# Four low-part subtractions of the recurrent mixer's weights made by GpSimd instead of VectorE, counted by VectorE

## The chip, the core and the metric

The kernel runs on one core of one Trainium2 chip. The metric is the device time of one execution in microseconds (us), taken as the median of several executions.

## The reference, cut to what matters

The whole computation is a stack of blocks over a sequence of 256 rows of width 1024. The part that the change touches is the recurrent mixer of the first layer. With `x` the normalised rows (256 x 1024), it computes:

```python
def recurrent_mixer(x, w_in, conv_w, conv_b, gate_a_w, gate_a_b, gate_x_w, gate_x_b, lam, w_out):
    y, r = jnp.split(x @ w_in, 2, axis=-1)
    y = jax.nn.gelu(y)
    r = causal_depthwise_conv(r, conv_w, conv_b)
    h = rg_lru(r, gate_a_w, gate_a_b, gate_x_w, gate_x_b, lam)
    return (y * h) @ w_out
...
    # rg_lru
    gate_a = jax.nn.sigmoid(block_diag_linear(xf, w_a, b_a))
    gate_x = jax.nn.sigmoid(block_diag_linear(xf, w_x, b_x))
    log_a = -LRU_C * gate_a * jax.nn.softplus(-lam)
    a = jnp.exp(log_a)
    mult = jnp.sqrt(-jnp.expm1(2.0 * log_a))
    bx = xf * gate_x * mult
    # h[t] = a[t] * h[t-1] + bx[t], a scan over the sequence
```

Ahead of it stands a feed-forward part (`in01`, `out01`) and behind it another one (`in02`, `out02`), then the second layer and two layers of an attention and mLSTM block.

## The kernel before, in words

**Weights in units.** All weight matrices are streamed once, in 456 units numbered in the order of use. A unit is a block of up to 4 x 128 rows and 256 columns, held as 128 partitions x 1024 elements. A ring of four slots holds it three times: `raw` (as loaded), `w_hi` (rounded by ScalarE, line 951) and `w_lo` = `raw` - `w_hi` (a subtraction on VectorE, line 1478). TensorE multiplies each unit in three products (`w_hi` by `x_hi`, `w_hi` by `x_lo`, `w_lo` by `x_hi`, lines 541 to 543), which is 24 matmuls of 256 columns, 12 for each of two output tiles. Two units that share their columns make a pair.

**The counts of the ring.** `lo_made` counts `w_lo` units in their order. TensorE's unit U waits until `lo_made` is U+1, and SyncE issues the load of unit U+4 then, since the slot of `raw` is free. `hi_made` counts `w_hi` units for the engine that subtracts. `unit_done` counts units that TensorE has finished; ScalarE waits for it before it writes `w_hi` of unit U+4 over that of unit U.

**The order on each engine is written out by hand**, and each engine runs its own list in order. In the mixer, `x @ w_in` (`rec_b` and `rec_a`) has 16 units, steps r = 0 to 15 of a loop over pairs p = 0 to 7. They are units 68 to 83; `rec_out` (`@ w_out`) is units 84 to 91. At step r ScalarE and VectorE make the high and the low part of unit 68 + r + 3 (`LEAD` = 3), and after the second unit of a pair VectorE takes its two tiles out of PSUM (`scaled`, line 1518, `work<-bank,rstd`). VectorE also has the mixer's own work: `conv1(p)` (lines 1631 and 1633, at r = 1, 3, 5, 7), `mult_squares` (line 1644, at r = 9 and 12), `scans` (products of line 1652, scans of line 1655, at r = 12, 13, 14), `outputs` (line 1661) and `lower` (`y_lo`, line 1489), from r = 14 on. TensorE's gate products (lines 631 and 632) stand after steps 3, 5, 7 and 8 and wait for `conv1`.

**GpSimd in the mixer** has one list: four products (line 1368) when ScalarE's gates are there, four squares of `rec_a` (line 1373, `a2_new`) behind ScalarE's exponentials (line 1059), and the same again for channels 4 to 7. Then it waits for `rec_out`. `mult_squares` on VectorE waits for `a2_new`, ScalarE's square root (line 1066) for `mult_squares`, the scans for the square root, and `rec_out`'s products for `y_hi` and `y_lo` of the eight channels: unit 84 for channels 0 to 3, unit 85 for channels 4 to 7.

Of the kernel before, what the change touches and what calls it, by code (L numbers as in the profile page):

```python
# [16 lines left out]
RING = 4  # L17
# [78 lines left out]
def plan():  # L96

    units, pairs, phases = [], [], {}

    def phase(name, src, layer, rows, cols):  # L100
        ub, pb = len(units), len(pairs)
        for c0 in cols:
            ks = []
            k = 0
            while k < rows:
                n = min(KU, rows - k) if rows - k != 6 else 3
                ks.append((k, n))
                k += n
            pairs.append([(len(units) + j, k0, n) for j, (k0, n) in enumerate(ks)])
            units.extend((src, layer, k0, n, c0) for k0, n in ks)  # L110
        phases[name] = (ub, pb, len(cols))

    wide = range(0, D, CU)
    for l in range(DEPTH):
        for f in (1, 2):
            gate_up = [c + s * FF for c in range(0, FF, CU) for s in (0, 1)]
            phase(f"in{l}{f}", f"ffn{f}_w_in", l, NC8, gate_up)
            phase(f"out{l}{f}", f"ffn{f}_w_out", l, NF, wide)
            if f == 1:
                m = ("rec", "sg")[l]  # L120
                phase(m + "_b", m + "_w_in", 0, NC8, [D + c for c in wide])
                phase(m + "_a", m + "_w_in", 0, NC8, wide)
                phase(m + "_out", m + "_w_out", 0, NC8, wide)
    for l in range(DEPTH):
        for n, c in (("kv", [C_KV]), ("mif", [C_MIF]), ("aq", [C_AQ + c for c in wide]),
                     ("mqk", [C_MQK + c for c in wide]), ("mv", [C_MV + c for c in wide]),
                     ("mo", [C_MO + c for c in wide]), ("ag", [C_AG + c for c in wide]),
                     ("mg", [C_MG + c for c in wide])):
            phase(f"{n}{l}", "w_in_2", l, NC8, c)
        phase(f"proj{l}", "w_out_2", l, 2 * NC8, wide)  # L130
    return units, pairs, phases


UNITS, PAIRS, PHASES = plan()
# [34 lines left out]
GATES_AT = (3, 5, 7, 8)  # L169


def build_stack(nc: bass.Bass, consts, x, ffn1_norm, ffn1_w_in, ffn1_w_out, mix_norm, ffn2_norm, ffn2_w_in, ffn2_w_out,
                rec_w_in, rec_conv_w, rec_conv_b, rec_gate_a_w, rec_gate_a_b, rec_gate_x_w, rec_gate_x_b, rec_lambda,
                rec_w_out, sg_w_in, sg_v_norm, sg_w_s, sg_b_s, sg_w_out, final_norm, meta_2, norm_g_2, w_in_2,
# [2 lines left out]
    fp32, fp32r = mybir.dt.float32, mybir.dt.float32r  # L177
    ALU, ACT = mybir.AluOpType, mybir.ActivationFunctionType
    MUL, ADD, SUB, MAX, MIN = ALU.mult, ALU.add, ALU.subtract, ALU.max, ALU.min
# [5 lines left out]
    with ExitStack() as ctx:  # L185
        def sb(name, shape, dt=fp32):
            return ctx.enter_context(nc.sbuf_tensor(name, shape, dt))

        def sem(name):
            return ctx.enter_context(nc.semaphore(name))  # L190
# [4 lines left out]
        raw = sb("raw", [P, RING, KU, CU])  # L195
        w_hi = sb("w_hi", [P, RING, KU, CU], fp32r)
        w_lo = sb("w_lo", [P, RING, KU, CU], fp32r)
# [30 lines left out]
        def region(slots, width=L):  # L228
            o = at[0]
            at[0] += slots * width  # L230
            assert at[0] <= WORK_SLOTS * L, at[0]
            return work[:, o:o + slots * width].rearrange("p (c n) -> p c n", n=width)
# [9 lines left out]
        decay = region(12, NC8)  # L242
# [55 lines left out]
        w_loaded = [sem(f"w_loaded{i}") for i in range(RING)]  # L298
        hi_made = sem("hi_made")
        lo_made = sem("lo_made")  # L300
        unit_done = sem("unit_done")
        first_done = sem("first_done")
        tile_read = sem("tile_read")
# [82 lines left out]
        def _(sp):  # L386
# [50 lines left out]
            def straight(name, first=0):  # L437
                ub, pb, npairs = PHASES[name]
                for pr in range(pb + first, pb + npairs):
                    for U, _, n in PAIRS[pr]:  # L440
                        src, l, k0, n, c0 = UNITS[U]
                        a = dram[src][l]
                        if name == "out01":

                            for dst, s_ in small[2 * (U - ub):2 * (U - ub) + 2]:
                                sp.dma_start(dst, s_).then_inc(sg_loaded, 16)
                        if name.startswith("mif"):

                            sp.wait_ge(lo_made, U - RING + 1)
                            for g in range(2):  # L450
                                sp.dma_start(raw[:, U % RING, 0:n, 32 * g:32 * g + 4],
                                             a[k0 * P:(k0 + n) * P, c0 + 4 * g:c0 + 4 * g + 4].rearrange(
                                                 "(k p) n -> p k n", p=P)).then_inc(w_loaded[U % RING], 16)
                            continue
                        load(U, a[k0 * P:(k0 + n) * P, c0:c0 + CU].rearrange("(k p) n -> p k n", p=P),
                             U - RING + 1 if U >= RING else None)

            def gate_up(name):

                ub, pb, _ = PHASES[name]  # L460
                src, l, _, _, _ = UNITS[ub]
                cols = dram[src][l].rearrange("(s k p) (f j n) -> s f j p k n", k=KU, p=P, f=2, n=CU)
                first = 1 if ub == 0 else 0

                def turn(i):
                    for j in range(4):
                        U = ub + j
                        wait = U - RING + 1 + 4 * i
                        load(U, cols[j % 2, j // 2, i], None if isinstance(i, int) and wait <= 0 else wait)

                if first:
                    turn(0)
                    parameters()
                with sp.Fori(first, FF // CU) as i:
                    turn(i)
# [840 lines left out]
        def _(pool):  # L1316
            nc.gpsimd.memset(ones[:, :], 1.0)
            nc.gpsimd.memset(epsc[:, :], EPS).then_inc(ones_set, 1)
            TT = nc.gpsimd.tensor_tensor
# [7 lines left out]
            def squares(src, wait, T0, done, chunks=NC8 - 1):  # L1327

                for c in range(chunks):
                    wait(c)  # L1330
                    if c == 0:
                        link(TT(sumsq[:, T0:L], src(c), src(c), MUL))  # L1332
                    else:
                        link(TT(sq[:, T0:L], src(c), src(c), MUL))  # L1334
                        i_ = TT(sumsq[:, T0:L], sumsq[:, T0:L], sq[:, T0:L], ADD)
                        if c < chunks - 1:
                            link(i_)
                        else:
                            i_.then_inc(done, 1)

            def h_squares(n, name, T0):

                pb = PHASES[name][1]
                if n:
                    pool.wait_ge(sum_done, n + (n == 7))
                squares(lambda c: h[:, c, T0:L], lambda c: pool.wait_ge(tile_read, 2 * pb + c + 1), T0, sq_done)

            def gate_scale(f):

                def turn(i):  # L1350
                    for m in range(2):
                        pool.wait_ge(silu_done, 22 * f + m + 1 + 2 * i)
                        TT(ffn_r[:, m, :], ffn_s[:, m, :], rstd[:, META:L], MUL).then_inc(gate_scaled, 1)  # L1353
                with pool.Fori(0, FF // CU) as i:
                    turn(i)
# [6 lines left out]
            gate_scale(0)  # L1362
            h_squares(1, "out01", META)

            for b in (0, 4):
                for c in range(b, b + 4):
                    pool.wait_ge(gates_sig, 2 * c + 2)
                    TT(rec_x[:, c, :], rec_x[:, c, :], rec_g[:, c, :], MUL).then_inc(gated_in, 1)
                if b:
                    pool.wait_ge(mult2, 4)  # L1370
                for c in range(b, b + 4):
                    pool.wait_ge(ax_new, c + 1)
                    TT(rec_s[:, c % 4, :], rec_a[:, c, :], rec_a[:, c, :], MUL).then_inc(a2_new, 1)
            h_squares(2, "rec_out", META)
            gate_scale(1)
            h_squares(3, "out02", META)
# [84 lines left out]
        def _(dve):  # L1461
            V = nc.vector
            TT, TS, STT = V.tensor_tensor, V.tensor_scalar, V.scalar_tensor_tensor
# [8 lines left out]
            def split_w(U, off=0):  # L1472

                if U >= NU:
                    return
                n, s = UNITS[U][3], U % RING
                dve.wait_ge(hi_made, U + 1 + off)
                TT(w_lo[:, s, 0:n, :], raw[:, s, 0:n, :], w_hi[:, s, 0:n, :].bitcast(fp32), SUB).then_inc(lo_made, 1)  # L1478
# [188 lines left out]
            r = 0  # L1667
# [114 lines left out]
            for l in range(DEPTH):  # L1782
# [297 lines left out]
                for ph in STREAM:  # L2080
                    pb = PHASES[f"{ph}{l}"][1]
                    for p in range(PHASES[f"{ph}{l}"][2]):
                        pr = pb + p
                        for j, (U, _, _) in enumerate(units_of(pr)):
# [9 lines left out]
                            if len(steps) == 1 and steps[0][0] == "ml" and steps[0][1][1] == 0:  # L2094
                                kind, n = steps[0]
# [32 lines left out]
            for g in (2, 3):  # L2128
                c0, n, _ = OUT_GROUPS[g]
# [30 lines left out]
```

## Time and profile before

| | us |
|---|---|
| three runs | 1537.73, 1538.11, 1539.76 |
| their median | 1538.11 |
| profiled execution, device time | 1541.56 |
| profiled execution, span from the first to the last instruction | 1539.8 |
| mean granted TensorE clock in it, share of full speed | 0.988 |

The profiled execution took 1.8 us more than its span, which is what lies around the instructions, and 3.5 us more than the median of the three runs. Starts in the trace are us from the start of the span; the mixer's 16 steps and the first two units of `rec_out` lie between 208 and 281 us. In the rows PE is TensorE, PEld its weight loads, DVE VectorE, ACT ScalarE, POOL GpSimd and SPq SyncE's DMA queue. Most of the mixer's tiles are regions of one tensor and are called `work` there.

### The profile page before, as it was taken

To read this page: it belongs to the slowest core of one execution; us is meant where nothing else is said; L and a number is where in the kernel's file an instruction comes from. 1 tells how busy PE (TensorE), PEld (TensorE's weight loads), DVE (VectorE), ACT (ScalarE), POOL (GpSimd) and SP (SyncE) were. 2 spreads that over 40 slices of the span, in tenths; PEclk is the share of its full clock that TensorE was granted. 3 is DMA by queue.
4 is the path that set the end of the run, shared out by engine and by line. 5 is a ranking of instruction groups with operands and counts; after the bars stand their busy time and mean duration, and the time that the engine had idled before them with its cause. 6 is when DMAs were issued, how large, how long until landed. Compare 5 with 4: busy or idle time off the path is not lost.

```text
span 1539.8 us, 31458 instructions
## 1 busy us (share of the span) xinstructions
PE 1488.7 (97%) x11949; PEld 1467.5 (95%) x11949; DVE 1050.3 (68%) x2004; ACT 768.7 (50%) x1276; POOL 293.7 (19%) x361
## 2 busy tenths in 40 slices
PE   7999998999999999999999998999999999999998
PEld 7999998999999999999999997899999999899898
DVE  6666578766655666557766655888768768976883
ACT  5444458554545554454554534446744453566442
POOL 4111112211111111113311112343200125331000
PEclk9999999999999999999999999899999999999999
DMA  6656744555555655555565554443333554334333
GB/s 203 188 177 199 243 161 132 164 182 176 184 175 185 191 178 179 170 184 165 163 188 176 179 180 126 126 120 97 97 111 109 164 139 137 101 106 117 109 121 121
DMA packets 245276, 239.66 MB, mean 156 GB/s; under 512 B 15160, under 2 KB 244392, under 8 KB 245048
## 3 DMA queue, kind: packets, MB, share of 16 engines
q1 hardware_dynamic: 245176, 238.29, 50.8%
q8 instruction: 67, 1.10, 0.3%
q14 instruction: 33, 0.27, 0.1%
HBM read 237.21 MB, written 1.05 MB: 155 GB/s over the span
## 4 chain that ended last, share of the span: by engine, by line
PE 85%; DVE 10%; ACT 2%; issue 2%; POOL 1%; DMA 0%; SPq 0%; DVEq 0%; ACTq 0%; POOLq 0%
PE bank L541 25%; PE bank L543 25%; PE bank L542 25%; DVE w_lo L1478 3%; PE bank L865 1%; PE bank L805 1%; PE bank L823 1%; PE bank L788 1%; ACT w_hi L951 1%; DVE work L1518 1%; DVE work L1633 1%; PE bank L871 1%; PE bank L881 1%; PE bank L804 0%; DVE rstd L1496 0%
## 5 line engine op out<-in xcount | busy, mean ns | idle before, releaser
L1478 DVE TENSOR_TENSOR w_lo<-raw,w_hi 128x1024 fp32r<-128x1024 f32 (+1 forms) x456 | 557.7, 1232 | 317.8 <-ACT w_hi L951 317.4
L541 PE MATMUL bank<-x_hi,w_hi 128*128 128x256 f32 (+1 forms) x2480 | 721.8, 291 | 7.1 <-DVE x_lo L1491 5.2
L543 PE MATMUL bank<-x_hi,w_lo 128*128 128x256 f32 (+1 forms) x2480 | 708.8, 286 | 0.0
L542 PE MATMUL bank<-x_lo,w_hi 128*128 128x256 f32 (+1 forms) x2480 | 708.3, 286 | 0.0
L951 ACT CAST w_hi<-raw 128x1024 fp32r<-128x1024 f32 (+1 forms) x456 | 466.2, 1031 | 273.5 <-PE bank L543 256.8
L541 PEld LDWEIGHTS bank<-x_hi,w_hi 128*128 128x128 f32 x2480 | 477.9, 193 | 10.3 <-issue 6.8
L542 PEld LDWEIGHTS bank<-x_lo,w_hi 128*128 128x128 f32 x2480 | 478.2, 193 | 1.0
L543 PEld LDWEIGHTS bank<-x_hi,w_lo 128*128 128x128 f32 x2480 | 477.5, 193 | 0.0
L541 PE MATMUL bank<-y_hi,w_hi 128*128 128x256 f32 (+1 forms) x1088 | 310.4, 285 | 8.4 <-DVE y_lo L1489 8.3
L543 PE MATMUL bank<-y_hi,w_lo 128*128 128x256 f32 (+1 forms) x1088 | 309.8, 285 | 0.0
L542 PE MATMUL bank<-y_lo,w_hi 128*128 128x256 f32 (+1 forms) x1088 | 309.7, 285 | 0.0
L541 PEld LDWEIGHTS bank<-y_hi,w_hi 128*128 128x128 f32 x1088 | 209.3, 192 | 9.4 <-DVE w_lo L1478 4.4
L543 PEld LDWEIGHTS bank<-y_hi,w_lo 128*128 128x128 f32 x1088 | 209.4, 193 | 0.0
L542 PEld LDWEIGHTS bank<-y_lo,w_hi 128*128 128x128 f32 x1088 | 209.2, 192 | 0.0
L1353 POOL TENSOR_TENSOR work<-work,rstd 128x256 f32<-128x256 f32 x88 | 63.6, 742 | 415.1 <-ACT work L987 415.1
L1518 DVE TENSOR_TENSOR work<-bank,rstd 128x256 f32<-128x256 f32 (+1 forms) x204 | 81.7, 422 | 17.1 <-PE bank L543 16.7
L997 ACT CAST y_hi<-work 128x256 f32 (+1 forms) x88 | 35.6, 408 | 90.3 <-DVE work L1534 90.2
L987 ACT ACTIVATE work<-work 128x256 f32<-128x256 f32 x88 | 36.1, 419 | 78.3 <-DVE work L1518 78.3
L1334 POOL TENSOR_TENSOR sq<-h 128x256 f32<-128x256 f32 (+1 forms) x48 | 33.5, 698 | 199.2 <-DVE h L1563 196.9
L958 ACT ACTIVATE x_hi<-h,par 128x256 fp32r<-128x256 f32 (+1 forms) x64 | 32.8, 514 | 70.2 <-DVE h L1563 62.7
L1491 DVE SCALAR_TENSOR_TENSOR x_lo<-h,par,x_hi 128x256 fp32r<-128x256 f32 (+1 forms) x64 | 36.3, 569 | 29.9 <-ACT x_hi L958 29.8
L1332 POOL TENSOR_TENSOR sumsq<-h 128x256 f32<-128x256 f32 (+1 forms) x8 | 4.9, 618 | 248.1 <-DVE h L1563 240.8
(269 smaller groups left out, 1250.4 us busy)
## 6 DMA issues: line engine op xcount, KB each, us to landing
raw<-in_ffn_w_in_dram SPq DMA_DIRECT2D x176, 512.0 KB, 3.7
raw<-in_w_in_dram SPq DMA_DIRECT2D x100, 512.0 KB, 3.6
raw<-in_ffn_w_out_dram SPq DMA_DIRECT2D x64, 512.0 KB, 4.2
raw<-in_w_out_dram SPq DMA_DIRECT2D x32, 512.0 KB, 3.8
raw<-in_ffn_w_out_dram SPq DMA_DIRECT2D x32, 384.0 KB, 3.1
raw<-in_rec_w_in_dram SPq DMA_DIRECT2D x16, 512.0 KB, 3.6
raw<-in_sg_w_in_dram SPq DMA_DIRECT2D x16, 512.0 KB, 3.5
raw<-in_rec_w_out_dram SPq DMA_DIRECT2D x8, 512.0 KB, 3.4
```

Source lines behind the costliest of these rows:

```text
L541: mm(acc, wh, xh, start=first and j == 0, stop=False)
L542: mm(acc, wh, xl, start=False, stop=False)
L543: i_ = mm(acc, wl, xh, start=False, stop=last and j == n - 1)
L951: nc.scalar.copy(w_hi[:, s, 0:n, :], raw[:, s, 0:n, :]).then_inc(hi_made, 1)
L958: i_ = activation(xview(dst, k, N), src, ACT.Copy, scale=scale)
L987: activation(ffn_s[:, m, :], ffn_t[:, m, :], ACT.Silu).then_inc(silu_done, 1)
L997: nc.scalar.copy(dst, ffn_h[:, m, :]).then_inc(act_hi, 1)
L1334: link(TT(sq[:, T0:L], src(c), src(c), MUL))
L1353: TT(ffn_r[:, m, :], ffn_s[:, m, :], rstd[:, META:L], MUL).then_inc(gate_scaled, 1)
L1478: TT(w_lo[:, s, 0:n, :], raw[:, s, 0:n, :], w_hi[:, s, 0:n, :].bitcast(fp32), SUB).then_inc(lo_made, 1)
L1491: i_ = STT(out=xview(dst_lo, k, N), in0=src, scalar=scale, in1=hi, op0=MUL, op1=SUB)
L1518: TT(dst, tile(pr, m, N), rstd[:, T0:L], MUL).then_inc(tile_read, 1)
```

## The change

GpSimd makes `w_lo` of four units: 78, 82, 84 and 86 (`POOL_LO`). It makes 78 after its first four squares, and the other three one behind the other after its second four squares. Each waits for that unit's `hi_made` and raises a new semaphore, `pool_lo`. VectorE leaves these four out, at steps r = 7, 11, 13 and 15. At the next step, before it subtracts the following unit, it waits for `pool_lo` and raises `lo_made` by a one-column memset on an unused column, so that `lo_made` still counts units in order. No DMA is added or removed, and no operation moves on TensorE, ScalarE or SyncE.

```diff
+POOL_LO = [PAIRS[PHASES["rec_b"][1]][0][0] + r for r in (10, 14, 16, 18)]
...
         lo_made = sem("lo_made")
+        pool_lo = sem("pool_lo")
...
+            def split_w(U):
+
+                n, s = UNITS[U][3], U % RING
+                pool.wait_ge(hi_made, U + 1)
+                TT(w_lo[:, s, 0:n, :], raw[:, s, 0:n, :], w_hi[:, s, 0:n, :].bitcast(fp32), SUB).then_inc(pool_lo, 1)
+
             for b in (0, 4):
...
                 for c in range(b, b + 4):
                     pool.wait_ge(ax_new, c + 1)
                     TT(rec_s[:, c % 4, :], rec_a[:, c, :], rec_a[:, c, :], MUL).then_inc(a2_new, 1)
+                for U in POOL_LO[1:] if b else POOL_LO[:1]:
+                    split_w(U)
...
                 if U >= NU:
                     return
+                if isinstance(off, int) and U + off in POOL_LO:
+                    return
+                if isinstance(off, int) and U + off - 1 in POOL_LO:
+                    dve.wait_ge(pool_lo, POOL_LO.index(U + off - 1) + 1)
+                    V.memset(decay[:, 10, 0:1], 0.0).then_inc(lo_made, 1)
                 n, s = UNITS[U][3], U % RING
                 dve.wait_ge(hi_made, U + 1 + off)
```

On GpSimd, its whole list in the mixer reads before:

```order
L1368 TENSOR_TENSOR work<-work 128x256 [waits gates_sig] x4
L1373 TENSOR_TENSOR work<-work 128x256 [waits ax_new] x4
L1368 TENSOR_TENSOR work<-work 128x256 [waits gates_sig] x4
L1373 TENSOR_TENSOR work<-work 128x256 [waits ax_new,mult2]
L1373 TENSOR_TENSOR work<-work 128x256 [waits ax_new] x3
```

and in the changed kernel, whose line numbers are up to 17 higher:

```order
L1378 TENSOR_TENSOR work<-work 128x256 [waits gates_sig] x4
L1383 TENSOR_TENSOR work<-work 128x256 [waits ax_new] x4
L1373 TENSOR_TENSOR w_lo<-raw,w_hi 128x1024 [waits hi_made]
L1378 TENSOR_TENSOR work<-work 128x256 [waits gates_sig] x4
L1383 TENSOR_TENSOR work<-work 128x256 [waits ax_new,mult2]
L1383 TENSOR_TENSOR work<-work 128x256 [waits ax_new] x3
L1373 TENSOR_TENSOR w_lo<-raw,w_hi 128x1024 [waits hi_made] x3
```

One subtraction of 1024 columns now stands between the first four squares and the next products, and three stand after the last squares.

On VectorE, the piece from steps r = 10 and 11 (units 81 and 82, the first row) to the first products of `scans` at r = 13 reads before:

```order
L1478 TENSOR_TENSOR w_lo<-raw,w_hi 128x1024 [waits hi_made] x2
L1518 TENSOR_TENSOR work<-bank,rstd 128x256 [waits first_done]
L1518 TENSOR_TENSOR work<-bank,rstd 128x256 [waits unit_done]
L1644 SCALAR_TENSOR_TENSOR work<-work 128x256 [waits conv_new,a2_new] x4
L1478 TENSOR_TENSOR w_lo<-raw,w_hi 128x1024 [waits hi_made]
L1652 TENSOR_TENSOR work<-work 128x256 [waits gated_in,mult_new] x4
L1655 SCALAR_TENSOR_TENSOR work<-work 128x256 [waits rec_bx] x4
L1478 TENSOR_TENSOR w_lo<-raw,w_hi 128x1024 [waits hi_made]
L1652 TENSOR_TENSOR work<-work 128x256 [waits gated_in,mult_new] x2
```

and in the changed kernel:

```order
L1495 TENSOR_TENSOR w_lo<-raw,w_hi 128x1024 [waits hi_made]
L1535 TENSOR_TENSOR work<-bank,rstd 128x256 [waits first_done]
L1535 TENSOR_TENSOR work<-bank,rstd 128x256 [waits unit_done]
L1661 SCALAR_TENSOR_TENSOR work<-work 128x256 [waits conv_new,a2_new] x4
L1492 MEMSET work 128x1 [waits pool_lo]
L1495 TENSOR_TENSOR w_lo<-raw,w_hi 128x1024 [waits hi_made]
L1669 TENSOR_TENSOR work<-work 128x256 [waits gated_in,mult_new] x4
L1672 SCALAR_TENSOR_TENSOR work<-work 128x256 [waits rec_bx] x4
L1669 TENSOR_TENSOR work<-work 128x256 [waits gated_in,mult_new] x2
```

The subtractions of units 82 and 84 are gone from it, and a memset with a wait stands ahead of unit 83's. Around steps 7 and 8, the end of `conv1(3)` is followed before by unit 79's subtraction:

```order
L1633 SCALAR_TENSOR_TENSOR work<-work,par 128x256 [waits dch]
L1633 SCALAR_TENSOR_TENSOR work<-work,par 128x256
L1478 TENSOR_TENSOR w_lo<-raw,w_hi 128x1024 [waits hi_made]
L1644 SCALAR_TENSOR_TENSOR work<-work 128x256 [waits conv_new,a2_new] x4
L1478 TENSOR_TENSOR w_lo<-raw,w_hi 128x1024 [waits hi_made]
```

and now by the memset for unit 78 and then by it:

```order
L1650 SCALAR_TENSOR_TENSOR work<-work,par 128x256 [waits dch]
L1650 SCALAR_TENSOR_TENSOR work<-work,par 128x256
L1492 MEMSET work 128x1 [waits pool_lo]
L1495 TENSOR_TENSOR w_lo<-raw,w_hi 128x1024 [waits hi_made]
L1661 SCALAR_TENSOR_TENSOR work<-work 128x256 [waits conv_new,a2_new] x4
L1495 TENSOR_TENSOR w_lo<-raw,w_hi 128x1024 [waits hi_made]
```

Unit 78's own subtraction stood at step 7 ahead of `scaled` and `conv1(3)`, and is gone from there.

## Rows read from the trace of the kernel before

**Rows 1.** The page: busy time by engine, the costliest group, the loads of `rec_out`.
```profile
PE 1488.7 (97%) x11949; PEld 1467.5 (95%) x11949; DVE 1050.3 (68%) x2004; ACT 768.7 (50%) x1276; POOL 293.7 (19%) x361
...
L1478 DVE TENSOR_TENSOR w_lo<-raw,w_hi 128x1024 fp32r<-128x1024 f32 (+1 forms) x456 | 557.7, 1232 | 317.8 <-ACT w_hi L951 317.4
...
raw<-in_rec_w_out_dram SPq DMA_DIRECT2D x8, 512.0 KB, 3.4
```

**Rows 2.** Stretches: us, busy PE, PEld, DVE, ACT, POOL; granted clock; DMA share, GB/s.
```profile
241.20:242.70 1.50, 0.03 (x1) 0.03 (x1) 1.45 (x4) 1.49 (x4) 0.11 (x1) 1.00 0.29 100
242.70:264.80 22.10, 22.10 (x176) 21.71 (x176) 18.39 (x30) 18.37 (x26) 6.67 (x8) 1.00 0.39 121
264.80:269.10 4.30, 0.04 (x2) 0.05 (x1) 4.30 (x11) 2.61 (x6) 0.00 (x0) 1.00 0.36 120
269.10:272.60 3.50, 3.50 (x17) 3.50 (x18) 3.50 (x10) 0.28 (x1) 0.00 (x0) 0.53 0.49 150
273.70:275.90 2.20, 0.03 (x1) 0.06 (x1) 1.15 (x4) 1.23 (x3) 0.00 (x0) 1.00 0.50 155
276.00:279.40 3.40, 3.34 (x15) 3.05 (x16) 2.74 (x7) 2.64 (x4) 0.00 (x0) 0.52 0.14 48
280.60:303.60 23.00, 23.00 (x194) 23.00 (x194) 16.57 (x24) 13.61 (x19) 9.23 (x13) 1.00 0.59 182
```

**Rows 3.** TensorE's timeline: start, us, instruction; idle before and releaser in brackets.
```profile
242.67 0.70 PE L631 MATMUL bank<-work 128*128 128x256 f32 x2 [1.56 <-DVE work L1633]
...
269.08 0.38 PE L541 MATMUL bank<-y_hi,w_hi 128*128 128x256 f32 x1 [4.26 <-DVE y_lo L1489]
...
275.87 0.35 PE L541 MATMUL bank<-y_hi,w_hi 128*128 128x256 f32 x1 [2.20 <-DVE y_lo L1489]
```

**Rows 4.** Timeline of VectorE, 235 to 277 us.
```profile
235.51 2.35 DVE L1478 TENSOR_TENSOR w_lo<-raw,w_hi 128x1024 fp32r<-128x1024 f32 x2
...
244.60 3.05 DVE L1644 SCALAR_TENSOR_TENSOR work<-work 128x256 f32<-128x256 f32 x4
...
254.30 1.39 DVE L1478 TENSOR_TENSOR w_lo<-raw,w_hi 128x1024 fp32r<-128x1024 f32 x1 [3.71 <-ACT w_hi L951]
...
256.27 1.42 DVE L1644 SCALAR_TENSOR_TENSOR work<-work 128x256 f32<-128x256 f32 x4
257.61 1.21 DVE L1478 TENSOR_TENSOR w_lo<-raw,w_hi 128x1024 fp32r<-128x1024 f32 x1
...
276.87 0.76 DVE L1489 TENSOR_TENSOR y_lo<-work,y_hi 128x256 fp32r<-128x256 f32 x2
```

**Rows 5.** Timeline of ScalarE, 247 to 255 us.
```profile
247.63 1.05 ACT L951 CAST w_hi<-raw 128x1024 fp32r<-128x1024 f32 x1 [1.15 <-PE bank L543]
...
251.61 1.71 ACT L1059 ACTIVATE work<-work 128x256 f32<-128x256 f32 x4
253.23 1.99 ACT L951 CAST w_hi<-raw 128x1024 fp32r<-128x1024 f32 x2
```

**Rows 6.** Timeline of GpSimd in the mixer.
```profile
238.29 2.61 POOL L1373 TENSOR_TENSOR work<-work 128x256 f32<-128x256 f32 x4 [5.21 <-ACT work L1059]
...
252.27 2.34 POOL L1373 TENSOR_TENSOR work<-work 128x256 f32<-128x256 f32 x4 [5.23 <-ACT work L1059]
```

**Rows 7.** Single instructions of GpSimd and VectorE around 243 us.
```profile
242.59 1.01 POOL L1368 TENSOR_TENSOR work<-work 128x256 f32<-128x256 f32 x1 [1.69 <-ACT work L1045]
...
242.93 1.75 DVE L1478 TENSOR_TENSOR w_lo<-raw,w_hi 128x1024 fp32r<-128x1024 f32 x1
...
243.56 1.72 POOL L1368 TENSOR_TENSOR work<-work 128x256 f32<-128x256 f32 x1
```

**Rows 8.** Durations by line, ns: lowest / median / highest.
```profile
L1368 POOL TENSOR_TENSOR work<-work x8: 736/926/1715, 229.5 to 246.1; 128x256 f32<-128x256 f32 x8
...
L1440 POOL TENSOR_TENSOR work<-work x18: 762/954/1847, 976.0 to 1304.5; 128x272 f32<-128x272 f32 x18
...
L1518 DVE TENSOR_TENSOR work<-bank,rstd x204: 396/420/443, 26.2 to 1488.7; 128x256 f32<-128x256 f32 x76, 128x272 f32<-128x272 f32 x26
```

## The prediction, made before the changed kernel ran

> **What bounds the kernel now.** The page comes first: TensorE is busy for 1488.7 of 1539.8 us, VectorE for 1050.3, GpSimd for 293.7, and the subtraction that the change moves is VectorE's largest group, 456 times 1.23 us [rows 1]. So the kernel as a whole is TensorE's, and work taken off VectorE is worth something only where TensorE waits for it. The table of stretches shows whether the mixer is such a place. TensorE works from 242.7 to 264.8 us without a gap, does nothing from 264.8 to 269.1, stands again from 273.7 to 275.9, and from 280.6 on has no gap (23.0 of 23.0 us) [rows 2]. Its own timeline names who ends these gaps: 1.56 us ended by `conv1` (line 1633), 4.26 and 2.20 us ended by `y_lo` (line 1489) [rows 3]. All three are VectorE. The granted clock belongs to the same picture: it is 1.00 in the gaps, and 0.53 and 0.52 in the 3.5 and 3.4 us after the gaps of 4.26 and 2.20 us, which is the lower of the two levels, 1.2 GHz; after the gap of 1.56 us it stays at 1.00 [rows 2, 3].
>
> So the end of the mixer is VectorE's chain, which ends with the last `y_lo` at 276.87 + 0.76 = 277.6 us [rows 4]; whatever moves that moment moves unit 86's start, and with it everything behind, since TensorE has no gap there. The chain passes once through other engines: unit 81's cast on ScalarE waited 1.15 us for TensorE (unit 77's end), the exponentials follow it, GpSimd's squares follow these, and `mult_squares` needs the squares [rows 5, 6]; VectorE's 3.71 us idle at 254.30 us is the wait for unit 82's cast, behind those exponentials [rows 4, 5].
>
> **What a w_lo on GpSimd costs.** On VectorE one takes 2.35 - 1.22 = 1.13 us of the chain (two in a row took 2.35) [rows 1, 4]. On GpSimd no row has 1024 columns. Products of two different inputs took 0.736 us at best for 256 columns and 0.762 for 272 [rows 8]. From the slope between these, 0.026 us for 16 columns, 1024 columns are 0.736 + 48 x 0.026 = 1.99 us; four times the short one is 2.94. I take the middle, 2.45 us. GPSIMD Engine Reference, section 3.1, in the Trainium skill gives 4497 ns for an fp32 add of 2048 columns; an estimate on the line between that and the 0.736 us of the row is 2.35 us, by which the sum below would be 0.4 us lower.
>
> **VectorE doesn't get that time for itself.** Around 243 us GpSimd's product ran from 242.59 to 243.60 us, and VectorE's subtraction, issued at 242.93, took 1.75 us instead of 1.22, to 244.68: it began 0.14 us before the product's end. GpSimd's next product, issued at 243.56, took 1.72 us instead of 0.74, to 245.28, so it began 0.14 us before the subtraction's end [rows 1, 7, 8]. The four `mult_squares` beside the further products took 3.05 us; the same four without GpSimd took 1.42 [rows 4]. An instruction of either engine thus keeps the other's out for its whole length less 0.14 us, and they take turns. Reads from PSUM don't take part: `scaled` took 0.443 us at most in 204 cases [rows 8]. SBUF — State Buffer, section "Who interferes with whom", in the Trainium skill says the same, that a VectorE instruction with two SBUF inputs and a GpSimd instruction that reads SBUF exclude each other for the whole instruction; what no row shows, and that page does, is that it also holds for a GpSimd instruction of 1024 columns. By that rule the change costs time, and it is the forecast here.
>
> So a unit moved to a place where VectorE has SBUF work ready takes 1.13 us off the chain and puts 2.45 - 0.14 = 2.31 us on it: 1.18 us net.
>
> **The four places.**
> - *Unit 78*, behind the squares that ended at 240.9 us [rows 6]. It meets `conv1(3)`, which now starts 1.13 us earlier but takes turns with the squares, and its last two operations then queue behind the subtraction. Net 1.2 us later for the gate products that began at 242.67 us. TensorE's gap grows from 1.56 to about 2.75 us. That is longer than the 2.20 us after which the clock was at 0.52, so I add the lower clock: 3.4 x (1 - 0.52) = 1.6 us at most, 1.4 taken, since part of it falls on waits [rows 2, 3]. Unit 77 ends later, so unit 81's cast, the exponentials and the second squares do: 2.6 us.
> - *Unit 82*, behind the second squares. Before, unit 83's subtraction began at 257.61 us. Now it needs the squares' end (254.61 before), 2.45 us on GpSimd, the last two `mult_squares` that queue behind it, 0.7, and the memset, 0.1: 254.61 + 3.25 = 257.86, or 0.2 us more than before, beside the shift that unit 78 caused [rows 4, 6].
> - *Unit 84*, made when ScalarE's cast is there, among `scans`, where VectorE has nothing but SBUF work: 1.2 us.
> - *Unit 86*, among `lower` and the last `scans`: 1.2 us.
>
> The memset is not in the rows; its cost lies between 0 and 0.3 us (a quarter of a subtraction of 1024 columns, for one column), and I count 0.1 once, inside unit 82's term; unit 86's memset stands behind the last `y_lo`.
>
> **Sum:** 2.6 + 0.2 + 1.2 + 1.2 = 5.2 us later. The profiled execution would go from 1541.56 to 1546.8 us; it stood 3.5 us above the median of the runs, so the median goes from 1538.11 to 1543.3. Bounds: with 1.99 us on GpSimd (4 x -0.46) and the clock kept (-1.4) it is +2.0, so 1540.1; with 2.94 (4 x 0.49) and three memsets of 0.3 on the path (+0.8) it is +8.0, so 1546.1.
>
> **New waits that should stay hidden.** The count for a moved unit comes one step later. Behind VectorE's wait for `pool_lo` are queued the next subtraction and all of VectorE's list. TensorE needs unit 78 about 5 us after that count and unit 86 only when unit 85 is done; the count for 86 comes right after the last `y_lo`, at 277.6 + 0.1 in before's frame, and unit 86 began at 280.6 [rows 2, 4]. On SyncE's queue the load of unit 90 waits for this count too; it lands 3.4 us later, at 281.1 [rows 1], 2.3 us before unit 86's end (280.6 + 2.9) lets ScalarE cast it. Were these covers gone, TensorE would wait for the difference.
>
> **Rivals.**
> - *Shorter: the long instruction doesn't keep VectorE out* (it lets go between pieces, or its turns fall into reads of PSUM). For it: no row has a GpSimd product this long. Against it: VectorE's 1024 columns kept GpSimd out for their whole length [rows 7]. Then units 78, 84 and 86 save 1.13 us each, 82 nothing (the second squares are there no earlier), two memsets cost 0.2: -3.2 us, 1534.9. It decides from a hold under 1.13 us an instruction. Chance 0.12.
> - *Milder:* `conv1(3)` gets its last turns before unit 78's subtraction, TensorE's gap stays under 2 us and the clock at 1.00. For it: in [rows 6] the turns were decided by a few tenths of a us. Then 0 + 0.2 + 1.2 + 1.2 = 2.6, and with the shorter GpSimd duration about 1.2: +2, 1540.1. Chance 0.25.
> - *A wait on the counts* (load of unit 90, or TensorE on a late count) that adds to the forecast: a few us, 1547 to 1550. Against it: the margins of 2.3 us and more above. Chance 0.05.
> - The forecast, +3 to +8 us, has 0.58.
>
> **How the numbers follow.** About 0.2% (3.1 us) is what a measurement of this kernel can tell from no change. Slower by more: 0.52 of the forecast's 0.58 (the rest lies at its lower end), all of the last rival and 0.05 of the milder one, 0.62. Faster by more: 0.10, most of the first rival. Same: 0.28. The likeliest case's own range is 1540.1 to 1546.1; the range over all reaches down to 1538.8, into the milder case, and leaves out the gain and the wait on the counts.
>
> **What would show it.** In the changed trace GpSimd's subtractions take 2 to 3 us; VectorE's `conv1`, product or `y_lo` beside each shows one instruction of 2 us or more instead of 0.4. The gap before the gate products at 242.67 us is about 2.75 us, with a clock near 0.5 behind it. The last `y_lo` ends at about 283 us instead of 277.6, and from there all is shifted alike. If VectorE's instructions beside GpSimd's keep their 0.4 us, the forecast is wrong at its root; if only the first of them does, it is the milder case.

## The result, and the profile after

| | before | changed |
|---|---|---|
| median of 7 executions, us | 1538.32 | 1542.71 |
| lowest and highest, us | 1537.31, 1540.39 | 1540.99, 1544.95 |
| profiled execution, device time, us | 1541.56 | 1540.99 |
| its span, us | 1539.8 | 1539.2 |

The changed kernel takes 1.0025 times as long (95% interval 1.0013 to 1.0036), which is 3.85 us more (2.0 to 5.5); the two medians are 4.39 us apart. The forecast was 1543.3 us, slower by more than 0.2%, in a range of 1538.8 to 1546.1 us.

The two profiled executions alone would say the opposite, 0.6 us less. So the time has to be read where the change is. A good ruler is the sum of squares of the norms on TensorE, a pair of matmuls (`sumsq` by ones) that comes once for each norm. One stands behind the second of the mixer's 16 steps (`rec_b`), the next one behind the first two units of `in02`, which follows `rec_out`, and two others stand far behind, in the attention and mLSTM block. Everything that the change touches lies between the first two. TensorE's timeline, before:

```profile
213.93 0.59 PE L567 MATMUL bank<-sumsq,ones 128*128 128x256 f32 x2
...
303.59 0.59 PE L567 MATMUL bank<-sumsq,ones 128*128 128x256 f32 x2
...
968.46 0.62 PE L902 MATMUL bank<-sumsq,ones 128*128 128x272 f32 x2
...
1256.18 0.62 PE L567 MATMUL bank<-sumsq,ones 128*128 128x272 f32 x2
```

and of the changed kernel:

```profile
213.60 0.59 PE L571 MATMUL bank<-sumsq,ones 128*128 128x256 f32 x2
...
306.74 0.59 PE L571 MATMUL bank<-sumsq,ones 128*128 128x256 f32 x2
...
972.38 0.62 PE L906 MATMUL bank<-sumsq,ones 128*128 128x272 f32 x2
...
1255.82 0.62 PE L571 MATMUL bank<-sumsq,ones 128*128 128x272 f32 x2
```

The distance between the first two, the ruler from here on, went from 303.59 - 213.93 = 89.66 to 306.74 - 213.60 = 93.14 us: +3.48 us, in the middle of what the timing says. The last stretch went from 287.72 to 283.44 us, where the change does nothing. In the seven profiles of the experiments below it lies between 283.4 and 284.9, so it was this one execution of the kernel before that lost some 3 to 4 us there. Its granted clock over this stretch was 0.98, that of the changed kernel 1.00. That hides the mixer's loss in the spans, and it may be most of the 3.5 us by which the profiled execution stood above the median.

The page of the changed kernel, the line that answers to [rows 1]:

```profile
PE 1486.0 (97%) x11949; PEld 1464.2 (95%) x11949; DVE 1055.6 (69%) x2004; ACT 768.0 (50%) x1276; POOL 306.4 (20%) x365
```

Four subtractions have gone from VectorE, 4 x 1.23 = 4.9 us of its own work, and VectorE is busy for 5.3 us more than before, not for 4.9 less. The timelines of GpSimd and of VectorE show why; the first four rows are GpSimd's new instructions for units 78, 82, 84 and 86, the second four what VectorE had issued beside each (`conv1`, `mult_squares`, a product of `scans`, `y_lo`), and the last row is the memset that counts unit 86:

```profile
241.06 2.53 POOL L1373 TENSOR_TENSOR w_lo<-raw,w_hi 128x1024 fp32r<-128x1024 f32 x1
255.11 2.59 POOL L1373 TENSOR_TENSOR w_lo<-raw,w_hi 128x1024 fp32r<-128x1024 f32 x1
262.81 2.54 POOL L1373 TENSOR_TENSOR w_lo<-raw,w_hi 128x1024 fp32r<-128x1024 f32 x1 [5.11 <-ACT w_hi L955]
271.12 2.38 POOL L1373 TENSOR_TENSOR w_lo<-raw,w_hi 128x1024 fp32r<-128x1024 f32 x1 [5.77 <-ACT w_hi L955]
```

```profile
241.30 2.57 DVE L1650 SCALAR_TENSOR_TENSOR work<-work,par 128x256 f32<-128x256 f32 x1
255.35 2.63 DVE L1661 SCALAR_TENSOR_TENSOR work<-work 128x256 f32<-128x256 f32 x1
263.08 2.55 DVE L1669 TENSOR_TENSOR work<-work 128x256 f32<-128x256 f32 x1
271.20 2.58 DVE L1506 TENSOR_TENSOR y_lo<-work,y_hi 128x256 fp32r<-128x256 f32 x1
...
280.29 0.06 DVE L1492 MEMSET work<- 128x1 f32 x1
```

Each time one VectorE instruction of 256 columns shows 2.55 to 2.63 us, where such instructions take about 0.4 [rows 4]. The memset takes 0.06 us. TensorE's timeline, which answers to [rows 3]:

```profile
241.43 0.70 PE L635 MATMUL bank<-work 128*128 128x256 f32 x2 [0.65 <-DVE work L1650]
...
243.92 0.70 PE L635 MATMUL bank<-work 128*128 128x256 f32 x2 [1.36 <-DVE work L1650]
...
244.70 0.47 PE L545 MATMUL bank<-x_hi,w_hi 128*128 128x256 f32 x1
...
270.76 0.56 PE L545 MATMUL bank<-y_hi,w_hi 128*128 128x256 f32 x1 [5.57 <-DVE y_lo L1506]
...
273.84 0.58 PE L545 MATMUL bank<-y_hi,w_hi 128*128 128x256 f32 x1 [0.82 <-DVE y_lo L1506]
...
278.58 0.55 PE L545 MATMUL bank<-y_hi,w_hi 128*128 128x256 f32 x1 [1.17 <-DVE y_lo L1506]
```

VectorE's subtraction of unit 83, the first behind the count of unit 82, and its last `y_lo` of the mixer:

```profile
258.25 1.21 DVE L1495 TENSOR_TENSOR w_lo<-raw,w_hi 128x1024 fp32r<-128x1024 f32 x1
...
279.58 0.76 DVE L1506 TENSOR_TENSOR y_lo<-work,y_hi 128x256 fp32r<-128x256 f32 x2
```

The table of stretches, which answers to [rows 2] (same columns):

```profile
241.40:244.00 2.60, 1.21 (x5) 0.76 (x5) 2.60 (x3) 2.24 (x6) 2.60 (x2) 1.00 0.00 0
...
270.70:273.80 3.10, 2.26 (x9) 2.00 (x9) 3.10 (x4) 0.34 (x1) 2.38 (x1) 0.50 0.84 270
273.80:282.20 8.40, 7.19 (x31) 6.77 (x32) 6.70 (x17) 3.87 (x7) 0.00 (x0) 0.50 0.12 35
...
282.20:306.70 24.50, 24.50 (x202) 24.50 (x202) 17.81 (x25) 13.74 (x19) 9.22 (x13) 0.98 0.60 186
```

From the norm sum ahead of it, the last `y_lo` ended after 276.87 + 0.76 - 213.93 = 63.70 us before [rows 4] and after 279.58 + 0.76 - 213.60 = 66.74 us now, 3.04 us later. The other 0.44 us of the 3.48 arise behind it: from the last `y_lo` to the next norm sum it is 25.96 us before and 26.40 now.

The subtraction of unit 83 divides the 3.04 us by place. It began 257.61 - 213.93 = 43.68 us behind the norm sum before [rows 4] and 258.25 - 213.60 = 44.65 now: 0.97 us for units 78 and 82 together, and 2.07 for 84 and 86.

The table of TensorE's waits between the two norm sums gives the same loss from TensorE's side. Before:

```profile
PE bank L541 <- DVE y_lo L1489: 6.5, 2, 4.3
PE bank L631 <- DVE work L1633: 2.2, 2, 1.6
```

and now:

```profile
PE bank L545 <- DVE y_lo L1506: 7.6, 3, 5.6
PE bank L635 <- DVE work L1650: 2.6, 3, 1.4
```

Waits grew from 8.7 to 10.2 us, 1.5 us. The rest is TensorE at the lower level of its clock, 1.2 GHz. Busy time times the missing share of the clock was 3.5 x 0.47 + 3.34 x 0.48 = 3.2 us before [rows 2] and is 2.26 x 0.50 + 7.19 x 0.50 + 24.5 x 0.02 = 5.2 us now, 2.0 us more. 1.5 + 2.0 makes the 3.5 us of the ruler.

### The profile page after: what moved, and what is told of

The parts are those of the page before. It is cut to its first block, busy times and chain, and to the rows that moved or that the text cites. A ratio compares the mean times of both kernels' runs of the same rounds, so it can differ in the third digit from the quotient of the medians.

```text
span 1539.2 us, 31462 instructions
## 1 busy us (share of the span) xinstructions
PE 1486.0 (97%) x11949; PEld 1464.2 (95%) x11949; DVE 1055.6 (69%) x2004; ACT 768.0 (50%) x1276; POOL 306.4 (20%) x365
## 3 DMA queue, kind: packets, MB, share of 16 engines
HBM read 237.21 MB, written 1.05 MB: 155 GB/s over the span
## 4 chain that ended last, share of the span: by engine, by line
PE 85%; DVE 10%; ACT 2%; issue 2%; POOL 1%; DMA 0%; SPq 0%; DVEq 0%; ACTq 0%; POOLq 0%
PE bank L545 25%; PE bank L547 25%; PE bank L546 25%; DVE w_lo L1495 2%; PE bank L869 1%; DVE work L1650 1%; PE bank L809 1%; PE bank L827 1%; PE bank L792 1%; ACT w_hi L955 1%; DVE work L1535 1%; PE bank L875 1%; PE bank L885 1%; PE bank L808 0%; DVE rstd L1513 0%
```

## The experiments

Seven kernels. Three of the quantities by which they are read come from one profile of each: the distance from the norm sum early in the mixer to the one early in `in02`, the end of the last `y_lo` counted from the first of these sums, and what is left from there to the second (the tail). The fourth is the timing against the kernel before; for the seven it is 6 to 11 executions against 25 or 29 of the kernel before on the same chip.

| kernel | distance, us | last `y_lo`, us | tail, us | time against before | 95% interval |
|---|---|---|---|---|---|
| before | 89.66 | 63.70 | 25.96 | | |
| changed | 93.14 (+3.48) | 66.74 (+3.04) | 26.40 | 1.0025 | 1.0013 to 1.0036 |
| e1_dummy_sub | 101.22 (+11.56) | 74.79 (+11.09) | 26.43 | 1.0064 | 1.0049 to 1.0079 |
| e2_dummy_write | 90.13 (+0.47) | 63.69 (-0.01) | 26.44 | 0.9999 | 0.9990 to 1.0008 |
| e3_only_78 | 90.71 (+1.05) | 64.40 (+0.70) | 26.31 | 1.0004 | 0.9994 to 1.0014 |
| e4_only_84_86 | 92.27 (+2.61) | 65.77 (+2.07) | 26.49 | 1.0006 | 0.9996 to 1.0016 |
| e5_quarters | 92.97 (+3.31) | 67.01 (+3.31) | 25.97 | 1.0024 | 1.0014 to 1.0034 |
| e6_defer | 87.93 (-1.73) | 61.41 (-2.29) | 26.52 | 0.9978 | 0.9969 to 0.9987 |
| e7_only_82 | 88.96 (-0.70) | 63.94 (+0.24) | 25.02 | 0.9999 | 0.9989 to 1.0008 |

### Only the GpSimd instructions, without the saving: e1_dummy_sub

Everything is as before, and GpSimd has in addition four subtractions of 1024 columns at the places of the changed kernel, of constants and into a scratch tile. Nobody waits for them, and VectorE still makes all of `w_lo`.

```diff
+                for U in POOL_LO[1:] if b else POOL_LO[:1]:
+                    pool.wait_ge(sg_loaded, SG_LOADS)
+                    pool.wait_ge(hi_made, U + 1)
+                    link(TT(ws_t[:, :, :].rearrange("p c n -> p (c n)"), con[:, 0:1024], con[:, 1024:2048], SUB))
```

> VectorE makes all weight low parts as before and no count changes; GpSimd makes, at the four places of the change, a subtraction of 1024 columns of constants into an unused tile, for which nobody waits (the output stays the reference's). Measure: the distance in the trace from the norm sum of rec_b to that of in02, 89.66 us in the kernel before and 93.14 in the changed one (+3.5). Port theory: each of the four takes about 2.3 us of port time and gives VectorE nothing back, so the cost is larger than the change's own, +6 to +10 us, and single VectorE instructions of 2.5 us stand beside GpSimd's. Rival, that the change costs by the count given a step late or by the wait for pool_lo: 0 within 0.5 us.

Measured: 1549.08 against 1539.62 us, +0.64%, and +11.56 us on the ruler. That is above the +6 to +10 us expected, and the rival's 0 is out. Instructions whose results nobody reads, with no count and no memset, cost the kernel 9.5 us by the medians, so subtractions on GpSimd cost time by themselves. In the changed kernel TensorE waits for no count either: its waits, above, are for `y_lo` and `conv1` alone. Timelines of GpSimd, TensorE and VectorE, and two stretches:

```profile
278.02 3.86 POOL L1380 TENSOR_TENSOR work<-con 128x1024 f32<-128x1024 f32 x1 [7.00 <-ACT w_hi L954]
...
244.99 1.22 PE L634 MATMUL bank<-work 128*128 128x256 f32 x2 [4.33 <-DVE work L1640]
...
259.12 1.37 DVE L1485 TENSOR_TENSOR w_lo<-raw,w_hi 128x1024 fp32r<-128x1024 f32 x1 [4.36 <-ACT w_hi L954]
...
263.96 1.22 DVE L1485 TENSOR_TENSOR w_lo<-raw,w_hi 128x1024 fp32r<-128x1024 f32 x1
...
268.79 3.32 DVE L1485 TENSOR_TENSOR w_lo<-raw,w_hi 128x1024 fp32r<-128x1024 f32 x1
...
278.35 0.75 DVE L1659 TENSOR_TENSOR work<-work 128x256 f32<-128x256 f32 x2
279.02 0.68 DVE L1662 TENSOR_TENSOR_SCAN work<-work 128x256 f32<-128x256 f32 x1
279.62 2.81 DVE L1662 TENSOR_TENSOR_SCAN work<-work 128x256 f32<-128x256 f32 x1
```

```profile
240.60:245.00 4.40, 0.07 (x2) 0.01 (x1) 4.33 (x5) 2.18 (x5) 3.97 (x3) 0.82 0.14 49
245.00:248.40 3.40, 3.40 (x9) 2.77 (x9) 2.81 (x6) 0.84 (x2) 0.38 (x1) 0.50 0.23 62
```

VectorE still makes unit 78's own low part here, so more of `conv1` is left when GpSimd's subtraction comes. TensorE's gap ahead of the gate products is 4.33 us instead of 1.56, and the granted clock in the 3.4 us behind it is 0.50. This is what the prediction feared of unit 78. It came about in this kernel, and not in the changed one.

The same rows say where the 11.09 us arise. VectorE's subtraction of unit 82 begins 259.12 - 213.48 = 45.64 us behind the norm sum instead of 40.37, that of unit 83 50.48 us instead of 43.68 [rows 4]: 5.3 us at unit 78's place and 1.5 at unit 82's. At unit 84's place a subtraction took 3.32 us instead of 1.2, at unit 86's a scan 2.81 instead of 0.68: 2.1 us each, the full price without the saving. Less the 1.13 us that the change saves, it is 1.0 us a place, half of the 2.07 for units 84 and 86.

### GpSimd busy for as long, but only writing: e2_dummy_write

The same places and waits, with three memsets of 1024 columns in place of each subtraction.

```diff
+                    for _ in range(3):
+                        link(nc.gpsimd.memset(ws_t[:, :, :], 0.0))
```

> As the first, but at each of the four places GpSimd only writes: three memsets of 1024 columns, about 2.9 us together. Port theory in the form that it is GpSimd's reads that exclude VectorE's instructions with two SBUF inputs: no VectorE instruction is longer than before, distance 89.7 within 0.5 us. If any SBUF access of GpSimd excludes VectorE: +6 to +10 us as with the subtractions.

Measured: 0.9999 times before. GpSimd's memsets and VectorE's `mult_squares` beside them:

```profile
254.34 2.99 POOL L1381 MEMSET work<- 128x1024 f32 x3
...
256.07 1.42 DVE L1652 SCALAR_TENSOR_TENSOR work<-work 128x256 f32<-128x256 f32 x4
```

The four `mult_squares` take 1.42 us, as they do without GpSimd [rows 4], and the last `y_lo` comes 0.01 us earlier than before. So a GpSimd that is busy writing doesn't hold VectorE up; one that reads SBUF does. SBUF — State Buffer, section "Who interferes with whom", in the Trainium skill says the same, that a VectorE instruction with two SBUF inputs contends with a GpSimd instruction that reads SBUF and not with one that only writes; e1 and e2 are the two halves of that sentence, at 11.09 and -0.01 us.

### One place at a time: e3_only_78, e7_only_82, e4_only_84_86

The changed kernel with a shorter list.

```diff
-POOL_LO = [PAIRS[PHASES["rec_b"][1]][0][0] + r for r in (10, 14, 16, 18)]
+POOL_LO = [PAIRS[PHASES["rec_b"][1]][0][0] + r for r in (10,)]
```

for unit 78, `(14,)` for unit 82 and `(16, 18)` for units 84 and 86, the last two with the list taken behind the second four squares alone.

> The change for unit 78 alone. The prediction's term was +2.6 us (1.2 by the port, 1.4 by the lower clock). The changed kernel's trace shows only one conv operation queued behind GpSimd, TensorE's gap split in 0.65 and 1.36 us and the clock at 1.00: by that the distance is 89.66 + 0.8 = 90.5. If the term was right after all and something else gave time back in the changed kernel: 92.3.

> The change for units 84 and 86 alone. Port theory: 2 x (2.31 - 1.13) = +2.4 less turns that fall well, so a distance of 91.8 to 92.1. Rival, that one long GpSimd instruction hurts only through the wait for pool_lo: 89.7 or less, since VectorE has two subtractions less.

> The change for unit 82 alone. The prediction's term was +0.2 us. From the difference of the others (3.48 - 1.05 - 2.61) it would be -0.2: a distance of 89.4 to 89.9. By the port's full price, 1.2: 90.8.

Measured by the end of the last `y_lo`: +0.70 us for unit 78, +0.24 for 82, +2.07 for 84 and 86. Their sum is 3.01 us, and the changed kernel with all four has 3.04: the places add up, and half the change costs two thirds of the whole. The distances missed what was expected in two of the three: 92.27 us is just above the 91.8 to 92.1 for units 84 and 86, and 88.96 is below the 89.4 to 89.9 for unit 82.

With unit 78 alone TensorE's gaps ahead of the gate products are those of the changed kernel:

```profile
241.42 0.70 PE L635 MATMUL bank<-work 128*128 128x256 f32 x2 [0.66 <-DVE work L1650]
...
243.91 0.70 PE L635 MATMUL bank<-work 128*128 128x256 f32 x2 [1.36 <-DVE work L1650]
```

The first half of the gate products runs between two gaps here, where before all of them ran in one go behind one gap, from 242.67 us [rows 3] to unit 77's first matmul:

```profile
244.32 0.47 PE L541 MATMUL bank<-x_hi,w_hi 128*128 128x256 f32 x1
```

The timings of the parts (1.0004, 0.9999, 1.0006) are each within 0.2% of before, and what the ruler says of each kernel (+1.05, -0.70 and +2.61 us are 1.0007, 0.9995 and 1.0017) lies in its interval or, the last, 0.0001 outside. Together they come to 1.0009, less than the 1.0025 of the whole; with intervals of 0.001 to each side that is no contradiction, and it is no proof of the sum either. That the places add up is shown by the profiles alone.

In e7 the distance is 0.70 us shorter than before, although its last `y_lo` comes 0.24 us later. The difference is in the tail, and the table of stretches says what it is:

```profile
276.00:279.40 3.40, 2.65 (x20) 2.48 (x21) 2.74 (x7) 2.62 (x4) 0.00 (x0) 1.00 0.29 97
```

Here the clock was back at 1.00 for the stretch in which it stood at 0.52 before [rows 2]. So the tail varies between 25.0 and 26.5 us among these profiles with the place of the stretch at 1.2 GHz, and a distance alone is not good to better than 1.5 us; the end of the last `y_lo`, which VectorE's chain sets, is the sharper measure, though it is read from one profile of each kernel.

### Shorter turns: e5_quarters

The changed kernel, with each GpSimd subtraction in four of 256 columns.

```diff
-                TT(w_lo[:, s, 0:n, :], raw[:, s, 0:n, :], w_hi[:, s, 0:n, :].bitcast(fp32), SUB).then_inc(pool_lo, 1)
+                for k in range(n):
+                    i_ = TT(w_lo[:, s, k, :], raw[:, s, k, :], w_hi[:, s, k, :].bitcast(fp32), SUB)
+                i_.then_inc(pool_lo, 1)
```

> The change with each of GpSimd's subtractions cut into four of 256 columns. Port theory: the port time is not less, 4 x (0.74 - 0.14) = 2.4 us a unit, and VectorE waits 0.6 us four times instead of 2.3 once; the distance between the norm sums stays at 92.5 to 94 us (93.1 with whole subtractions). Rival, that the length of one hold is what hurts: below 91.5.

Measured: 1.0024 times before, 1.0014 to 1.0034, like the changed kernel. GpSimd's timeline for unit 86, VectorE's around the count of unit 82, and TensorE's:

```profile
271.98 3.38 POOL L1374 TENSOR_TENSOR w_lo<-raw,w_hi 128x256 fp32r<-128x256 f32 x4 [5.10 <-ACT w_hi L955]
...
259.21 1.22 DVE L1497 TENSOR_TENSOR w_lo<-raw,w_hi 128x1024 fp32r<-128x1024 f32 x1 [2.01 <-issue]
259.23 0.06 DVE L1494 MEMSET work<- 128x1 f32 x1
...
259.35 0.39 PE L545 MATMUL bank<-x_hi,w_hi 128*128 128x256 f32 x1 [0.97 <-DVE work L1494]
```

With pieces, several VectorE instructions wait for a quarter each instead of one for the whole, and the hold isn't shorter in sum. Beside unit 86's pieces four `y_lo` took 1.95 us instead of the 1.43 of the kernel before, two products 1.82 instead of 0.75 and two scans 1.80 instead of 1.26, together 2.1 us more; beside the whole subtraction of the changed kernel the four `y_lo` took 3.58, which is 2.15 more. But the unit is ready later: VectorE stood 2.01 us ahead of the memset that counts unit 82 (and as long ahead of unit 78's), and TensorE waited 0.97 us for this count (line 1494). This is the wait on the counts that the prediction held for hidden, with its cover taken away.

### The other way round: e6_defer

The runs say that the path is VectorE's list up to the last `y_lo`, and that TensorE needs units 85 and 86 only later. So here VectorE keeps all subtractions, as before, and two stand further behind: that of unit 85 behind the last pair's `scaled`, that of unit 86 behind the last `y_lo`. GpSimd has nothing new.

```diff
                         outputs(range(4, 6))
-                    split_w(U + LEAD)
+                    if r < 14:
+                        split_w(U + LEAD)
...
+            split_w(U + LEAD - 1)
             lower(range(4, 6))
             outputs(range(6, 8))
             lower(range(6, 8))
+            split_w(U + LEAD)
```

> A version of the kernel before, without GpSimd's help: VectorE makes the low part of unit 85 after the last scaled tiles of the mixer, where it waits 1.05 us for ScalarE's y_hi, and that of unit 86 after the last y_lo, instead of ahead of them. If VectorE's chain to the last y_lo is the bound of the mixer's end, the distance falls by 1.1 (unit 86) and 1.0 (unit 85), to 87.2 to 87.9 us, and the time by 1.5 to 3 us. If the loads or casts that follow the later counts bind instead, it stays at 89 or more.

Measured: 1536.34 against 1539.48 us, 0.9978 times before (0.9969 to 0.9987), faster than the kernel before and the changed one; the distance of 87.93 us is at the upper end of what was expected. Timelines of VectorE and TensorE:

```profile
274.47 0.76 DVE L1489 TENSOR_TENSOR y_lo<-work,y_hi 128x256 fp32r<-128x256 f32 x2
275.15 3.49 DVE L1478 TENSOR_TENSOR w_lo<-raw,w_hi 128x1024 fp32r<-128x1024 f32 x3
```

```profile
267.82 0.36 PE L541 MATMUL bank<-y_hi,w_hi 128*128 128x256 f32 x1 [3.12 <-DVE y_lo L1489]
...
273.48 0.36 PE L541 MATMUL bank<-y_hi,w_hi 128*128 128x256 f32 x1 [1.13 <-DVE y_lo L1489]
```

TensorE's gap ahead of `rec_out` is 3.12 us instead of 4.26, by the 1.14 us of one subtraction, and the gap at the second four channels 1.13 instead of 2.20 [rows 3]. The last `y_lo` ends 2.29 us earlier, which is two subtractions. On the ruler 1.73 us of it are left, since the tail is 0.56 us longer: TensorE stood at 0.50 from 275.9 to 279.2 us here. The timing shows 3.1 us between the medians, 2.0 at its interval's near end; where the difference to the 1.73 comes from, one profile can't say.

## Why the prediction was right, and where it was not

- **The root, right.** "An instruction of either engine keeps the other's out for its whole length less 0.14 us", carried over from 256 columns to 1024. The instruction beside each subtraction took 2.55 to 2.63 us, GpSimd's 2.38 less 0.14 plus its own 0.4. e1 and e2 show that it is GpSimd's reading subtractions that cost, and not a busy GpSimd or a late count. The first rival, with a gain of 3.2 us, is out.
- **2.45 us for 1024 columns on GpSimd.** 2.38 us where it had nothing ahead of it (unit 86); the estimate of 2.35 us that stands beside it was the nearer.
- **Units 84 and 86, 2.4 us.** Measured 2.07 (e4).
- **Unit 82, 0.2 us.** Measured 0.24 (e7). The changed kernel's own 0.97 us at unit 83, less unit 78's 0.71, gives 0.26: the working was right too.
- **Unit 78, 2.6 us: the step that failed.** It measured 0.70 (e3). The prediction put 1.2 us on the gate products, since "its last two operations then queue behind the subtraction", and 1.4 us on a lower clock behind a gap of "about 2.75 us". Only the last operation of `conv1(3)` queued behind it, at 241.30 us. With the last but one done, the first half of the gate products ran at 241.43 us, in what was a gap before. TensorE's idle time was cut into 0.65 and 1.36 us, the clock stayed at 1.00 (that it did so because of the cut is not shown), and unit 77, which began at 244.32 us before and begins at 244.70 now, is 0.38 + 0.33 = 0.71 us late once the different starts of the two norm sums are taken off. The prediction treated four gate products as one event that waits for all of `conv1`; the program has a wait for each half.
- **"From there all is shifted alike": 0.44 us off.** The sum had no term for the clock behind the last `y_lo`. TensorE is busy without a pause from there to the second norm sum, before and now, and the table of stretches gives the granted clock, before and then now:

```profile
277.63:303.59 25.96, 25.96 (x210) 25.96 (x211) 19.01 (x27) 15.04 (x21) 9.23 (x13) 0.96 0.53 163
```

```profile
280.34:306.74 26.40, 26.40 (x210) 26.40 (x211) 19.16 (x28) 15.20 (x21) 9.22 (x13) 0.94 0.59 180
```

What the lower clock took is 25.96 x 0.04 = 1.0 us before and 26.40 x 0.06 = 1.6 now, and e7, at 1.00 throughout, had a tail of 25.02 us. To within the rounding of these shares the 0.44 us are the clock's; whether they belong to the change or to this one execution is open, since the tails of the other profiles vary by more.
- **Waits on the counts, right as hidden**: TensorE waited for none. e5 shows their price when the cover goes.
- **The sum.** 5.2 us predicted; the ruler says 3.48, the timing 3.85 (2.0 to 5.5). What came about lies between the forecast and the rival called milder: its clock of 1.00, its sign and nearly its size (2.6 us), but 0.70 us at unit 78 where it had nothing. That the median of 1542.71 came out 0.6 us from the forecast owes something to chance: the sum had 1.7 us too much against the ruler, but the medians stand 4.39 us apart, 0.9 more than the ruler says, and the median before, over seven executions, was 0.2 us above the one over three that the forecast started from.

## What to carry to other kernels

Work that reads SBUF is not taken off VectorE by giving it to GpSimd while VectorE has instructions with two SBUF inputs ready: each costs VectorE nearly the length that it has on GpSimd, here some 2.2 us for 1.13 saved. If TensorE waits for VectorE, first ask which of VectorE's instructions ahead of the awaited one serve a later consumer, and put them behind it; that alone gave 0.2% here. And when one execution's profile contradicts the timing, compare distances between the same two instructions, phase by phase, before believing either.

## What was unexpected

- **The turns are not strict.** In e1 a GpSimd instruction that was issued at 278.02 us ended at 281.88, so with its own 2.38 us it began only about 279.5. Meanwhile VectorE started two products and a scan (278.35, 279.02) back to back, and only the second scan was held, taking 2.81 us. SBUF — State Buffer, section "SBUF: two separate sides", in the Trainium skill says that whichever of a GpSimd instruction and a VectorE one with two SBUF inputs starts first gets the pair for the whole instruction. That doesn't describe this: by the profile GpSimd's had started before all three. Where VectorE's instructions follow each other without a gap, GpSimd can be passed over. What decides it was not settled.
- **Scans take part** in the exclusion: the one of 2.81 us takes 0.68 otherwise.
- **The clock after idle time in pieces.** Gaps of 0.65 and 1.36 us with the first half of the gate products between them left it at 1.00; one gap of 2.20 us was followed by 0.52 [rows 2, 3], one of 4.33 us (e1) by 0.50. But in e6 TensorE stood at 1.00 from 273.5 to 275.8 us and at 0.50 from 275.9 to 279.2, with no gap longer than 1.13 us since 267.8. So the length of a single gap, from which the prediction reasoned at unit 78, doesn't tell by itself.
